# Two-block transformer step on one Trainium2 core: where the product keys' norm and turning are done, and how many first products stand ahead of the queries

## What is computed

```python
gates = jax.nn.sigmoid(h @ w_gate + b_gate).reshape(B, S, 3, D)
merged = gates[:, :, 0] * y_sb + gates[:, :, 1] * y_dil + gates[:, :, 2] * y_mem
x = x + merged @ w_out                       # the gate stage ends here
h2 = rms_norm(x, g_ffn)                      # the norm that the change moves
x = x + peer_ffn(h2, w_peer_q, peer_subkeys, peer_u, peer_v)
```

## Time and profile before

| | us |
|---|---|
| three runs, lowest / median / highest | 2895.64 / 2897.2 / 2902.78 |
| the profiled execution, device time | 2895.71 |
| its span, first to last instruction | 2893.8 |
| TensorE busy | 2790.9 (96% of the span) |
| VectorE busy | 2038.1 (70%) |
| ScalarE busy | 1380.3 (48%) |
| mean granted TensorE clock | 0.986 of full speed |

### The profile page before, as it was taken

The page is one execution under the profiler, slowest core; times in us unless marked ns, Lnnn a source line. Parts: engine busy times, 40 slices in busy tenths (PEclk is TensorE's granted clock), DMA queues, the critical chain, the costliest instruction groups (busy, mean ns, idle before and its releaser), DMA issues. The chain is left out here.

```text
span 2893.8 us, 36724 instructions
## 1 busy us (share of the span) xinstructions
PE 2790.9 (96%) x13965; PEld 2367.8 (82%) x13965; DVE 2038.1 (70%) x3268; ACT 1380.3 (48%) x2185; POOL 413.1 (14%) x293
## 2 busy tenths in 40 slices
PE   7999999899999999989999999999999899999999
PEld 5756888578888688968788789999999888888887
DVE  4476533388888625776653688898887868888886
ACT  4336522277777615765432433367666543233332
POOL 0000000000100100000000000211112335544552
PEclk9999999799999999999999999999999999999999
DMA  4100262557677621121242324677778979999996
GB/s 168 52 23 1 83 172 90 233 204 298 260 294 273 235 109 52 60 97 45 92 138 81 141 104 135 226 253 266 271 271 327 358 279 391 392 391 392 393 389 261
DMA packets 165854, 600.48 MB, mean 208 GB/s; under 512 B 15792, under 2 KB 87088, under 8 KB 137392
## 3 DMA queue, kind: packets, MB, share of 16 engines
q1 hardware_dynamic: 106928, 436.08, 41.3%
q0 software_dynamic: 41472, 138.45, 12.9%
q10 hardware_dynamic: 17280, 23.60, 2.2%
HBM read 563.96 MB, written 71.86 MB: 220 GB/s over the span
## 5 line engine op out<-in xcount | busy, mean ns | idle before, releaser
L2730 POOL DMA_INDIRECT RG<-in_un,EI x128 | 182.6, 1427 | 1242.9 <-DVE EI L2982 842.4
L2730 POOL DMA_INDIRECT RG<-in_vn,EI x128 | 184.1, 1439 | 257.6 <-DVE X L2744 230.7
L3101 PE MATMUL bank<-VH,GL 128*128 128x512 f32 x768 | 208.5, 393 | 0.4 <-DVE GL L2796 0.4
L3097 PE MATMUL bank<-VH,GH 128*128 128x512 f32 x768 | 208.0, 392 | 0.0
L2744 DVE SCALAR_TENSOR_TENSOR X<-RG,DG,X 128x1024 f32<-128x1024 f32 x128 | 164.2, 1283 | 42.6 <-DMA RG<-in_vn,EI 38.7
L2741 DVE CUSTOM_DVE_ANT_0 RG<-RG,HR 128x1024 f32<-128x1024 f32 x128 | 156.5, 1223 | 36.1 <-DMA RG<-in_un,EI 35.4
L2711 PE MATMUL bank<-HTl,UH0r 128*128 128x384 f32 x512 | 175.8, 343 | 0.2 <-ACT UH0r L2696 0.2
L2711 PE MATMUL bank<-HTl,UH1r 128*128 128x384 f32 x512 | 175.9, 344 | 0.0
L2712 PE MATMUL bank<-HTh,UH1r 128*128 128x384 f32 x512 | 172.0, 336 | 0.0
L2712 PE MATMUL bank<-HTh,UH0r 128*128 128x384 f32 x512 | 171.4, 335 | 0.0
L3101 PEld LDWEIGHTS bank<-VH,GL 128*128 128x128 f32 x768 | 144.1, 188 | 33.2 <-DVE GL L2796 0.9
(11 more groups left out here) (718 smaller groups left out, 7695.6 us busy)
## 6 DMA issues: line engine op xcount, KB each, us to landing
UR<-in_u SPq DMA_DIRECT2D x64, 1024.0 KB, 7.1
VR<-in_vn SPq DMA_DIRECT2D x32, 2048.0 KB, 10.0
UP<-in_wup SPq DMA_DIRECT2D x22, 2048.0 KB, 8.1
DN<-in_wdn SPq DMA_DIRECT2D x32, 1024.0 KB, 7.0
wspill<-VR SPq DMA_DIRECT2D x12, 2048.0 KB, 8.3
aspill<-GA ACTq DMA_DIRECT2D x120, 192.0 KB, 5.3
W<-in_weights SPq DMA_DIRECT2D x10, 2048.0 KB, 11.2
HT<-in_wup SPq DMA_DIRECT2D x10, 2048.0 KB, 7.5
```

The source lines that it names most:

```text
L2730: e.indirect_dma_start(RG[q % RR], None, d["un" if what == "u" else "vn"][:, :], off).then_inc(*row_in[q % RR].up(16))
L3097: e.matmul(bk, r(gh[:, a, t]), r(vh[:, a, :]), start=g == 0 and a == 0, stop=False)
L3101: e.matmul(bk, r(gl[:, a, t]), r(vh[:, a, :]), start=False, stop=False)
```

## The change

Five things change together.

1. Blocks 0 to 2 are squared, rooted and scaled inside the gate stage, each as soon as its second half is added to X: ScalarE after `x_add(5 + tb)`, VectorE after the additions of units 4, 5 and 6. The rows go to tiles of their own (XR).
2. The first pair's weights (UR0) are loaded by SyncE behind LO1w in the gate stage, and split there by ScalarE (after the root of block 0) and VectorE (after block 1's rows). `load_u(0)`, `act_u(0)` and `dve_u(0)` go from the next stage.
3. The next stage begins with 24 transposes of blocks 0 to 2, high and low parts of 384 columns a bank, and no dummy products. Product 0 waits for the low parts one by one.
4. Block 3 is squared, rooted and scaled in that stage, turned by 8 transposes behind product 1, and its high and low parts are written ahead of the loop of steps. Queries wait for them.
5. `FIRSTS` begins with 3, then seven times 1, then 2 (before: eight times 1, then 3). So step 0 has products 0, 1 and 2, step 8 has two instead of three, and one less is left for the 34 steps ahead of the last 8.

```diff
@@ Late.sync, Late.act, Late.dve
                     e.dma_start(self.OUT[1][0], w_src(48)).then_inc(*self.out_in[1].up(16))
+                    e.dma_start(UR0[0], d["u"][0][:, 0:2].rearrange("p a k n -> p (a k n)")).then_inc(*u_in[0].up(16))
...
                     self.act_out_split(e, 1)
+                    for tb in range(3):
+                        e.wait_ge(*self.x_add(5 + tb))
+                        act_square(e, tb)
+                        act_norm_root(e, tb)
+                        if tb == 0:
+                            e.wait_ge(*u_in[0](16))
+                            e.activation(r(UH0), UR0[0], ACT.Copy).then_inc(*f_hi.up(1))
...
                         e.tensor_tensor(o, o, bank[OUT_BANK[u]], ALU.add).then_inc(*self.x_add.up(1))
+                        if 4 <= u < 7:
+                            e.wait_ge(*self.x_add(u + 1))
+                            dve_norm_rows(e, u - 4)
+                        if u == 5:
+                            e.wait_ge(*f_hi(1))
+                            e.tensor_tensor(r(UR0[1]), UR0[0], UH0, ALU.subtract).then_inc(*f_lo.up(1))
...
+            def act_square(e, tb):
+                e.activation(XR[tb], X[:, tb, :], ACT.Square, accum_out=s3[:, tb:tb + 1]).then_inc(*s_sq.up(1))
+            def act_norm_root(e, tb):
+                e.wait_ge(*s_var(tb + 1))
+                e.activation(o3[:, tb:tb + 1], v3_[:, tb:tb + 1], ACT.Sqrt).then_inc(*s_root.up(1))
+            def dve_norm_rows(e, tb):
+                c = slice(tb, tb + 1)
+                e.wait_ge(*s_sq(tb + 1))
+                e.tensor_scalar(v3_[:, c], s3[:, c], 1.0 / 1024, EPS, ALU.mult, ALU.add).then_inc(*s_var.up(1))
+                e.wait_ge(*s_root(tb + 1))
+                dve_newton(e, o3[:, c], v3_[:, c], t3_[:, c])
+                e.tensor_scalar(XR[tb], X[:, tb, :], o3[:, c], None, ALU.mult).then_inc(*s_rows.up(1))
@@ pe_first
                 for k in range(8):
+                    if q == 0:
+                        e.wait_ge(*s_lo(k + 1))
@@ FIRSTS
-                FIRSTS = [1.0] * 8 + [3.0] + [1.0] * 14 + [1.2] * 14
+                FIRSTS = [3.0] + [1.0] * 7 + [2.0] + [1.0] * 14 + [1.2] * 14
@@ SyncE
-                        load_u(e, 0)
@@ TensorE
-                        warm(e, 6, 7)
-                        norm.pe_turn(e)
-                        e.wait_ge(*n_keptV(4 + 4))
-                        warm(e, 5, 0)
-                        e.wait_ge(*n_keptV(4 + 8))
+                        for k in range(8):
+                            if k >= 6:
+                                e.wait_ge(*s_lo(k - 5))
+                            for tb in range(3):
+                                i = e.transpose(bank[TURN_BANK[k]][:, span(tb)], XR[tb][:, span(k)], ident)
+                            i.then_inc(*s_turn.up(1))
                         for step in range(NQ + NM):
                             for q in firsts(step):
                                 pe_first(e, q, bank[place(q)], last_at(q))
+                                if q == 1:
+                                    e.wait_ge(*s_rows(4))
+                                    for p in range(2):
+                                        for j in range(4):
+                                            i = e.transpose(bank[4 + p][:, span(j)], XR[3][:, span(4 * p + j)], ident)
+                                        i.then_inc(*s_turn.up(1))
+                            if step == 0:
+                                e.wait_ge(*s_lo(10))
@@ ScalarE
-                        norm.act_sums(e)
-                        norm.act_root(e)
+                        for k in range(8):
+                            e.wait_ge(*s_turn(k + 1))
+                            e.activation(r(HH_[:, k, 0:NT3]), bank[TURN_BANK[k]][:, 0:NT3], ACT.Copy, scale=gain[:, k:k + 1]).then_inc(*s_hi.up(1))
+                        act_square(e, 3)
+                        act_norm_root(e, 3)
                         act_q(e, 0)
-                        for k in range(8):
-                            e.wait_ge(*n_turn(24 + k + 1))
-                            e.activation(r(HH_[:, k, :]), bank[k], ACT.Copy, scale=norm.gain[:, k:k + 1]).then_inc(*n_keptA.up(1))
-                        act_u(e, 0)
+                        for p in range(2):
+                            e.wait_ge(*s_turn(9 + p))
+                            for j in range(4):
+                                k = 4 * p + j
+                                i = e.activation(r(HH_[:, k, NT3:512]), bank[4 + p][:, span(j)], ACT.Copy, scale=gain[:, k:k + 1])
+                            i.then_inc(*s_hi.up(1))
@@ VectorE: in the same order low parts of 384 columns, dve_norm_rows(e, 3), dve_q(e, 0), low parts of block 3, then
-                        e.tensor_tensor(HR3, HR3, norm.xn[:, 3, :], ALU.mult).then_inc(*g_mul.up(1))
-                        dve_u(e, 0)
+                        e.tensor_tensor(HR3, HR3, XR[3], ALU.mult).then_inc(*g_mul.up(1))
```

More of the change, by code:

```diff
@@ L2649, in dve @@
                         e.tensor_tensor(o, o, bank[OUT_BANK[u]], ALU.add).then_inc(*self.x_add.up(1))
-            MIX_AT = {(1, 3): range(4), (2, 4): range(4, 6)}
+                        if 4 <= u < 7:
[4 more added lines that the diff above has]
+                            e.tensor_tensor(r(UR0[1]), UR0[0], UH0, ALU.subtract).then_inc(*f_lo.up(1))
+            MIX_AT = {(1, 3): range(4), (2, 4): range(4, 6)}
+            XR = [nc.alloc_sbuf_tensor_at(f"XR{b}", [128, 1024], F32, offset=101504 + 4096 * b)[:, :] for b in range(4)]
+            UH0 = nc.alloc_sbuf_tensor_at("UHe", [128, 2048], F32, offset=150656)[:, :]
+            UR0 = [nc.alloc_sbuf_tensor_at(f"URe{x}", [128, 2048], F32, offset=158848)[:, :] for x in ("w", "l")]
+            s3, o3, v3_, t3_ = (nc.alloc_sbuf_tensor_at(f"{n}3", [128, 4], F32, offset=228480 + 32 * k)[:, :] for k, n in enumerate(("ss", "rt", "va", "tm")))
+            s_sq, s_var, s_root, s_rows, f_hi, f_lo = sems("s_sq s_var s_root s_rows f_hi f_lo", True)
+            u_in = [sem(f"u_in{n}", True) for n in range(3)]
+            def act_square(e, tb):
[10 more added lines that the diff above has]
+                e.tensor_scalar(XR[tb], X[:, tb, :], o3[:, c], None, ALU.mult).then_inc(*s_rows.up(1))
             SPLIT_AT = {0: 1, 2: 2, 1: 3}
@@ L2675, in program @@
             HH_, HL_ = (sb(n, [128, 8, 512], cu) for n in ("HTh", "HTl"))
-            UR = [sb2(f"UR{n}", [128, 2048], cu) for n in range(3)]
-            UH = [sb2(f"UH{n}", [128, 2048], cu) for n in range(2)]
+            assert nc.sbuf_base == 150656
+            sb("UHUR", [128, 4096], cu)
+            UR = [UR0] + [sb2(f"UR{n}", [128, 2048], cu) for n in (1, 2)]
+            UH = [(None, UH0), sb2("UH1", [128, 2048], cu)]
             row_in = [sem(f"row_in{n}", True) for n in range(RR)]
             r_used, r_gelu, r_gate, r_ids, g_in, g_mul = sems("r_used r_gelu r_gate r_ids g_in g_mul")
-            u_in, v_in = [sem(f"u_in{n}") for n in range(3)], [sem(f"v_in{n}") for n in range(2)]
+            v_in = [sem(f"v_in{n}") for n in range(2)]
             ld, ws_done, ga_done = sem("ld"), [sem(f"ws_done{n}") for n in range(2)], [sem(f"ga_done{n}") for n in range(4)]
-            f_hi, f_lo, f_mm, f_gelu = sems("f_hi f_lo f_mm f_gelu")
+            f_mm, f_gelu = sems("f_mm f_gelu")
             v8 = lambda a: a.rearrange("p (k n) -> p k n", k=8)
@@ L2821, in program @@
                 QS = [RG[3][:, span(n, 256)] for n in range(3)]
-                norm = Norm(cx, "ffn2", 2, 3, None, "ffn2", rows=RowsOf(RG))
+                gain = gg("ffn2")
+                s_turn, s_hi, s_lo = sems("s_turn s_hi s_lo")
+                TURN_BANK = (2, 3, 4, 5, 6, 7, 2, 3)
                 p_wh, p_wl, p_q, p_qt, p_sc, p_sk, p_top = sems("p_wh p_wl p_q p_qt p_sc p_sk p_top")
@@ L3237, in _ @@
                     def _(e):
-                        norm.dve_rows(e)
-                        dve_q(e, 0)
-                        for k in range(8):
-                            e.wait_ge(*n_keptA(4 + k + 1))
-                            e.scalar_tensor_tensor(r(HL_[:, k, :]), bank[k], norm.gain[:, k:k + 1], HH_[:, k, :], ALU.mult, ALU.subtract).then_inc(*n_keptV.up(1))
+                        for k in range(8):
+                            e.wait_ge(*s_hi(k + 1))
+                            e.scalar_tensor_tensor(r(HL_[:, k, 0:NT3]), bank[TURN_BANK[k]][:, 0:NT3], gain[:, k:k + 1], HH_[:, k, 0:NT3],
+                                                   ALU.mult, ALU.subtract).then_inc(*s_lo.up(1))
+                        dve_norm_rows(e, 3)
+                        dve_q(e, 0)
+                        for p in range(2):
+                            e.wait_ge(*s_hi(9 + p))
+                            for j in range(4):
+                                k = 4 * p + j
+                                i = e.scalar_tensor_tensor(r(HL_[:, k, NT3:512]), bank[4 + p][:, span(j)], gain[:, k:k + 1], HH_[:, k, NT3:512], ALU.mult, ALU.subtract)
```

(4 more changed lines are left out.)

## The result

The changed kernel is slower: 2908.85 us, median of 6 runs (2903.84 to 2909.11), against 2897.61 for the kernel before (6 runs, 2895.64 to 2902.78). The ratio is 1.0044, with a 95% interval of 1.0031 to 1.0056. The forecast was 2893.8 with a range to 2902. The profiled execution took 2908.23 (before: 2895.71), its span is 2906.4.

The account below looks back on a forecast made before the run. From the seam on, TensorE's own work was taken to set the end nearly everywhere, transfers in the last 34 shared steps. 8.3 - 1.7 - 1.8 + 0.8 - 2.2 = 3.4 us gained: 2893.8 us, range 2885 to 2902.

Parts of the forecast that it names:

- The gate stage: Norm of blocks 0 to 2 hides in idle time there; last addition stays in place, cost 0 (upper bound 4.5 late).
- The seam: Between gate stage and queries: three first products instead of one, 8.3 us gained; product 2 waits 5.8, clock takes 1.7.
- Product 14's wait: Steps 8 to 36: TensorE waits 3.2 us instead of 1.4 for product 14's low part, -1.8 (bounds -3 and 0).
- The 0.8 us wait at step 36: TensorE's wait for the choice hung on a split that shifts by one product; its end gains +0.8 (bounds 0 and 0.8).
- The prediction's own signs of being wrong: Product 2 right behind the transposes; gate stage additions late; waits for one-hots changed by more than 5 us.
- The last 34 shared steps: Ahead of the last 8: transfers set the pace, so one product fewer gives 2.2 of 4.16 us not back (-2.2).
- The rival of the second long wait: Second gather falls behind in the 34 steps, 7.9 us more: 2901.7; twice over 2909.6; chance 0.14 together.
- The rule on table loads: Skill page adds a drain of about 1.38 us to a load's 1.28; product 2 1.4 later, sum 2.0.
- the rival of a longer pause: A pause about as long as the load (1.3 us) at ScalarE's table switch ahead of product 2: 2895.1; chance 0.03.

Follow-up runs that it names:

- Experiment 6: Changed kernel with product 0's Gelu and pair 1's split ahead of block 3's parts, pair 1 loaded second, `FIRSTS` as changed: 2899.32 us, ratio 1.0006.
- Experiment 2: Kernel before with four products instead of three in step 8, nothing of the seam: 2917.17 us, ratio 1.0073.
- experiment 4: Changed kernel, VectorE doing the choice's last part of blocks 0 to 2 ahead of the next pair's split, `FIRSTS` unchanged: 2892.94 us, ratio 0.9984.
- experiment 1: Changed kernel with one product instead of two in step 8 (11 by step 9, as in the kernel before): 2887.29 us, ratio 0.9969.
- experiment 5: Changed kernel with two products instead of three in step 0, two in step 8 (11 by step 9): 2885.2 us, ratio 0.9956.
- experiment 7: Changed kernel with one product in step 8, and product 0's Gelu and pair 1's split ahead of block 3's parts: 2883.82 us, ratio 0.9950.

## Why the prediction was wrong

**The gate stage: right.** The additions stand at 1590.00 and 1594.63, block 1 held the third back as worked out, and the fourth was on time. Square ran behind Sqrt without a load of a table (the root at 1581.50 is followed by the copy and by block 1's square at 1584.47, with no load between).

**The seam: right.** Product 1's end, 1607.36, was put at 1609.8 - 2.55 = 1607.25. Product 2 waited 5.5 us (5.8 forecast), and took 5.96 us instead of 4.16 (1613.75 to 1619.71), 1.8 lost to the clock (1.7 forecast). The two products were worth 8.3 less 0.9, 7.4 us, against a forecast of 6.6. Experiment 6 shows both terms to be real: without them 7.3 us come back by the marks, 9.5 by the medians.

**Product 14's wait: right**, 3.2 us; but the clock fell behind it, too, which was not in the sum (1.7 us).

**The step that failed** is "The 0.8 us wait at step 36 hung on a split that shifts by one product: **+0.8** (bounds 0 and 0.8)". I looked at the split that the wait hung on, product 40's, and not at the one that comes after it. Product 40's stays in step 35, ahead of part 12, where VectorE now waits 0.42 us for it instead of 3.00. But product 42's came from step 37, behind the choice's last part, to step 36, ahead of it, and there TensorE is the one that waits. In the trace of the changed kernel product 41 ends at 1888.9. From there a Gelu with its store, the table load ahead of the exponential, the exponential, the high part 1.90, the split 2.29 and the last part 0.9 had to pass, 7.4 us in all with their small overlaps, while TensorE had one product of 4.16: it waited 3.3. And it happened three times, since blocks 1 and 2 have such a step each; in the kernel before they showed no wait, so I had no row for them and gave them no term. Instead of +0.8, the term is -10.2 for the waits (11.0 less 0.8) and -5.9 for the clock behind them (1.7, 2.5 and 1.7). With product 14's 1.8 and 1.7 that makes 19.6 us for the shift. Experiment 2 shows the shift's whole price without the seam, 19.2 us, experiment 4 the price of the order alone, 15.9. The prediction's own signs of being wrong did not show this: none of the three came true.

**The last 34 shared steps** were the second miss, by size: the stretch was counted to return 1.9 of a product's 4.16, bounds 0 and 4.16 lost. It became 1.9 us longer with a product fewer, so 6.1 were not returned (+1.9 and 4.16). Of these, 1.7 are the slow clock behind block 2's SEL and belong to the first miss; 4.4 remain against the 2.2 forecast, and in these steps TensorE's waits for one-hots grew by 2.5 us and the clock was lower for longer behind them. How much of this is the missing product is open: with the same product count the stretch came out at 193.5, 193.2, 194.7 and 197.0 us (the kernel before, experiments 1, 5 and 7), so executions differ there by nearly as much as a product. The rival of the second long wait had the right sign, but neither this place nor this cause.

**The rule on table loads.** The table load ahead of product 0's Gelu took 1.28 us, from 1611.82 to 1613.10, with the Gelu at 1613.11 and the high part's end at 1611.80 before it. So the rival of a longer pause did not come. The drain of 1.38 us that "ScalarE: Activation LUTs" of the Trainium skill adds in "What ACT_TABLE_LOAD costs" does not show here.

## What to carry to other kernels

Where two engines follow lists in which every second item brings extra work, moving the count by one moves that extra work everywhere behind. Ahead of such a change, write out for each step in which one engine waits for the other what stands ahead of the awaited instruction, before and after, also where the trace shows no wait now. And look for the part of the schedule where another resource sets the pace, and count work moved out of it at little or nothing: here, by the marks of single executions, two products fewer gave back 1.9 of 8.3 us, and two more cost at most 1.4.

## What the runs showed of the hardware

In the changed kernel the granted clock fell to 0.50 at each of the three waits for SEL (3.3, 4.0 and 3.7 us), and it stayed low when TensorE was working again: after the wait that ended at 2025.11 it was still 0.50 in the slice to 2029. That cost 1.7, 2.5 and 1.7 us on top of the waits. I had counted waits of this length at their own length.

The price does not follow the length of the wait. Behind the 5.5 us at the seam 1.7 us were lost, and behind the 7.9 us in the kernel before 1.8. Behind product 14's 3.2 us it was 1.7 in the changed kernel and nothing in experiment 4, where the clock stayed at 1.00 throughout behind the same wait. Behind the same product's 1.4 us in the kernel before nothing was lost.

The second products, which ran beside 391 GB/s of transfers (the kernel before, 2500 to 2600 us), took 4 gathered rows more, that is 8 gathers, without a loss, and not 8 rows: with these TensorE waited 8.1 us there for low parts, where it had waited 0.7.
